# The memory's rows for its mean square: four pieces during RWKV instead of two loads during the memory's split

## The chip, the core and the metric

The kernel runs on one core of one Trainium2 chip. A core has five engines, each with its own instruction queue: TensorE (PE, matrix products; PEld is its weight load), VectorE (DVE), ScalarE (ACT), GpSimd (POOL) and SyncE (SP, which here issues most DMAs). They meet through semaphores. Sixteen DMA engines move data between the chip's memory (HBM) and the on-chip buffer (SBUF); products land in PSUM banks. The metric is the time of the device in microseconds (us), lower is better, as a median over runs.

## What is computed

Two transformer blocks over 256 tokens of width 2048. The first has four token mixers (gated DeltaNet, mLSTM, RG-LRU, RWKV-7) and a gated feed-forward; the second has three attention branches, one of which reads a memory `mem` of 256 rows. The part that the change touches is the norm of that memory, and what runs beside it:

```python
def rms_norm(x, w):                       # over the last axis, eps 1e-6
    return x * rsqrt(mean(x * x) + eps) * w

def second_block(x, mem, ...):
    mem_n = rms_norm(mem, norm_mem_g)     # (256, 2048)
    ...
    mkv = einsum('bmd,de->bme', mem_n, w_mem_kv)
    mk, mv = split(mkv, 2)

def mlstm(u, ...):
    qk, v, o_raw, i_raw, f_raw = split(u, ...)
    qk = silu(causal_conv(qk, conv_w))    # conv over time, width 4
    q, k = heads(qk)                      # 4 heads, k scaled by 128 ** -0.5
    ...                                   # gated attention in chunks, then a norm per head
```

RG-LRU needs `softplus(-lambda)`; RWKV-7 needs, for two halves of its heads, a unit triangular matrix inverted. The gate of RWKV is `sigmoid(g_lo) @ g2`, with `g2` of 128 by 512.

## The kernel before

**The projections set the order.** Nearly all of TensorE's work is weight blocks times activations in split precision: each weight is cut into a high part (`ringH`, made by ScalarE, L1362) and a low part (`ringL`, raw minus high, made by VectorE, L1983), and three products are added up (L682/L683, or L653 to L655). A weight unit of 1 MB comes by a DMA of SyncE (L3039) into one of 3 buffers `raw`; a half of 1024 columns goes into one of 4 slots of `ringH` and `ringL`. In this part a half lasts TensorE some 2.8 us. The blocks have names: `w0` to `w6` feed RWKV, `m0` to `m3` mLSTM, `g...` DeltaNet.

**The mixers are woven in.** Each engine runs a generator per stage (`norm`, `mem`, `rwkv`, `mlstm` and so on), and `course` advances them by so many projection steps for each `yield`. The leading engine records at which step each of its yields falls, and the other engines follow these records. So a stage with more yields moves all stages behind it in its lane to later projection steps, on every engine. During RWKV a second lane, `beside_rwkv`, runs at the same pace: `scan` with `mem` (the memory's split into `memSt`, stored to `mem_hold` in four DMAs of 1 MB by SyncE, L3090), then `fold`, `lambda`, `mlstm`.

**What the stages hold.** `fold` is the memory's mean square: GpSimd loads the memory's 256 rows (in `mem`, two DMAs of 1 MB, L2923) into `memk`, which lies in the buffer of RG-LRU's input `gU`; ScalarE squares each of the two 128 x 2048 tiles and adds them up (L1554); VectorE scales the sum (L2230), ScalarE takes the root (L1490), VectorE the reciprocal (L2233), TensorE spreads it over the partitions (L775), VectorE copies it out of PSUM (L2237). `lambda` is a chain of small VectorE operations (L2195 to L2218) on 128 x 4 values behind an absolute value and an exponential of ScalarE (L1562, L1564). `mlstm` is a convolution for Q and one for K (ScalarE taps L1679 and Silu L1684; VectorE three L2515 per head), then for each of four heads a broadcast (L1089) and a product K Q (L1098); ScalarE copies the first out (L1716), VectorE takes differences (L2543), ScalarE the exponential (L1719), VectorE masks it (L2546, L2547) and multiplies it by the product (L2550); then TensorE's L1107 and L1111, whose bank VectorE frees at L2566; in the end a norm (L885).

**RWKV** goes through two halves of its heads. In each: sigmoids (ScalarE L1618), decays (VectorE L2368 to L2386, ScalarE L1624 to L1627), a root (ScalarE L1588) and its reciprocal (VectorE L2333), a broadcast (TensorE L902), then products and five levels of the inversion (TensorE L841, then L849 and L854; VectorE L2296, L2304, L2309). The products of all these stages share a ring of four PSUM banks, `ps4` to `ps7`: whoever takes a bank waits until the product that was in it four takes earlier has been read. VectorE's first shift of RWKV (L2349) stands behind `e.wait_ge(s_mh[2], 16)` (L2344), the landing of the third store to `mem_hold`, since RWKV's scratch overwrites the `memSt` it is stored from. The drain of block `.m0` (ScalarE) and the two memsets of GpSimd (L2932, L2933) wait for both squares.

Of the kernel before, what the change touches and what calls it, by code (L numbers as in the profile page):

```python
# [254 lines left out]
def beside_rwkv(L):  # L255
    scan = L.stage("scan")
    next(scan)
    yield
    for _ in L.stage("mem"):
        next(scan, None)  # L260
        yield
    yield from scan
    yield from L.stage("fold")
    yield from L.stage("lambda")
    while not L.done("m0"):
        yield
    yield from L.stage("mlstm")
# [50 lines left out]
def program(nc, I, out):  # L318
    ctx = ExitStack()
    with ctx:  # L320
# [23 lines left out]
        def v2(o, n):  # L344
            return AR[:, o:o + n]
# [50 lines left out]
        s_c, s_an, s_i, s_p, s_h, s_w, s_w2, s_o = (sem(f"s_{n}") for n in ("c", "an", "i", "p", "h", "w", "w2", "o"))  # L396
        s_xr, s_m, s_w3 = ([sem(f"s_{n}{k}") for k in range(2)] for n in ("xr", "m", "w3"))
        s_mt = sem("s_mt")
        s_x = [sem(f"s_x{k}") for k in range(6)]
        s_first = [sem(f"s_first{k}") for k in range(3)]  # L400
# [44 lines left out]
        sqs = v3(GU, 16, T)  # L445
        memk = v3(GU, 2, D)
        wsm = v3(SC + 8192, 16, 16)
# [143 lines left out]
        def tensor(e, S, ring, lane):  # L591
# [176 lines left out]

            def fold(L):
                for _ in range(4):  # L770
                    yield
                e.wait_ge(*me_v.at("r"))
                b = take("me", "r")
                for tt in range(2):
                    t = m1(b[:, ts(tt)], rm[:, tt:tt + 1].broadcast_to([128, 128]), ident, tt == 0)  # L775
                t.then_inc(*me_p.tick("r"))
                for _ in range(2):
                    yield
# [544 lines left out]
            def attB(L):  # L1323
# [10 lines left out]
            course(lane(unit, {  # L1334
                "norm": norm, "gates": gates, "scan": scan, "fold": fold, "lambda": lam, "stat2": stat2, "mem": mem, "rwkv": rwkv, "mlstm": mlstm, "gdn": gdn,
                "rglru": rglru, **{f"mix{m}": split(4) for m in range(4)}, **{f"split1.{q}": split1(q) for q in range(4)},
# [3 lines left out]
        def scalar(e, S, ring, lane):  # L1340
# [23 lines left out]
            def drain(B):  # L1364
                tag, what, bk = B.tag, kind[B.tag], PS[2 * (B.n % 2):2 * (B.n % 2) + 2]
                e.wait_ge(*use.at(half_end[tag] - 1))
                if tag == ".m0":
                    e.wait_ge(*me_a.at("ss", 1))
                    for g in range(4):
                        e.wait_ge(s_mh[g], 16)  # L1370
# [179 lines left out]

            def fold(L):
                for tt in range(2):
                    e.wait_ge(s_m[tt], 16)
                    act(memk[:, tt, :], memk[:, tt, :], ACT.Square, accum_out=small[:, 116 + tt:117 + tt]).then_inc(  # L1554
                        *me_a.tick("ss", tt))
                    yield
                root(me_v, me_a, rm)
                yield
# [376 lines left out]
            def final(L):  # L1935
# [10 lines left out]
            course(lane(unit, {  # L1946
                "norm": norm, "scan": scan, "mem": mem, "fold": fold, "lambda": lam, "rwkv": rwkv, "mlstm": mlstm,
                "gdn": gdn, "rglru": rglru,
# [8 lines left out]
        def vector(e, S, ring, lane):  # L1957
# [267 lines left out]

            def fold(L):
                yield
                yield
                e.wait_ge(*me_a.at("ss", 1))
                tsc(rm, small[:, 116:118], 1.0 / D, 1e-6, MUL, ADD).then_inc(*me_v.tick("ms"))  # L2230
                yield
# [628 lines left out]
            def attB(L):  # L2860
# [6 lines left out]
            course(lane(unit, {  # L2867
                "norm": norm, "gates": gates, "scan": scan, "mem": mem, "fold": fold, "lambda": lam, "rwkv": rwkv, "mlstm": mlstm, "gdn": gdn, "rglru": rglru,
                **{f"mix{m}": split("mix", nS, lambda k: mix[:, k, :], range(4 * m, 4 * m + 4)) for m in range(4)}, "stat1": stat1,
# [6 lines left out]
        def gpsimd(e, S, ring, lane):  # L2876
            use, drain_a, drain_v, pool, nx_a, me_a = (S[n] for n in ("use", "drain_a", "drain_v", "pool", "nx_a", "me_a"))
            nx_p, me_v, nx_v, gd_p, gd_a, gd_v, rg_a, rg_v, ml_v, sp_v, at_v = (
                S[n] for n in ("nx_p", "me_v", "nx_v", "gd_p", "gd_a", "gd_v", "rg_a", "rg_v", "ml_v", "sp_v", "at_v"))
            tr_p, st_a, st_v = S["tr_p"], S["st_a"], S["st_v"]  # L2880
# [37 lines left out]

            def mem(L):
                yield  # L2920
                e.wait_ge(*nx_p.at("r"))
                for tt in range(2):
                    e.dma_start(memk[:, tt, :], I["mem_2"][0, ts(tt), :]).then_inc(s_m[tt], 16)  # L2923
                yield

            def fold(L):
                for _ in range(5):
                    yield
                e.wait_ge(*me_a.at("ss", 1))
                for g in range(4):  # L2930
                    e.wait_ge(s_mh[g], 16)
                e.memset(mU[:, :, 0:3], 0.0).then_inc(*pool.tick("mU"))  # L2932
                e.memset(gU[:, :, 0:3], 0.0).then_inc(*pool.tick("gU"))  # L2933
                yield

# [92 lines left out]

            course(lane(unit, {"begin": begin, "mem": mem, "fold": fold, "gdn": gdn, "rglru": rglru, "gains": gains, "xf": finals, **{f"split2.{q}": split2(q) for q in range(4)}, "mk": mk, "mv": mv, "xc": xc}))

# [182 lines left out]
```

## Time and profile before

| | us |
|---|---|
| median of 3 runs | 2418.83 |
| lowest and highest | 2418.06, 2420.80 |
| the profiled execution | 2422.39 |
| its span | 2420.60 |

| engine | busy us | share |
|---|---|---|
| TensorE | 2391.7 | 99% |
| VectorE | 1451.6 | 60% |
| ScalarE | 1131.5 | 47% |
| GpSimd | 104.1 | 4% |

The span goes from the first to the last instruction in the trace; the execution's own time is 1.8 us more. TensorE is busy nearly throughout, so what counts is the little time in which it waits, and what its matmuls cost while the chip grants it less than the full clock. In the profile's rows a wait is given with the instruction that ended it.

### The profile page before, as it was taken

Reading aid. Unit: us, or ns where it says so; the run is one execution under the profiler, and the core shown is the slowest. Engines: PE = TensorE matmul, PEld = TensorE weight load, DVE = VectorE, ACT = ScalarE, POOL = GpSimd, SP = SyncE. Lnnn points to the kernel's source line nnn. Section 1 sums busy time; section 2 is a strip of 40 time slices with the busy share of each in tenths; the row PEclk is TensorE's granted clock in tenths of the full one; section 3 lists DMA queues with packets and bytes.
Section 4 is the critical chain, followed back from the end, with each engine's and each line's share of the span. In section 5 each row is a group of like instructions: output and inputs, shape, how many; then the busy total and the mean of one; then the engine's idle time right before and its main releaser. Section 6 shows DMA issues by size and latency. Waiting matters only on the chain.

```text
span 2420.6 us, 32301 instructions
## 1 busy us (share of the span) xinstructions
PE 2391.7 (99%) x13432; PEld 1990.9 (82%) x13432; DVE 1451.6 (60%) x1860; ACT 1131.5 (47%) x1425; POOL 104.1 (4%) x81
## 2 busy tenths in 40 slices
PE   9999999999999999999999999999999999999998
PEld 7777888978888888888888888888888888888887
DVE  6777657678755555555555565555555655555555
ACT  6635435563554444434443464445444455444444
POOL 1000001320000000000000040000000000000000
PEclk9999999999999999999999999999999999999999
DMA  9633334645555555555555566555445544555564
GB/s 298 224 123 122 123 123 162 234 162 184 196 192 184 185 190 188 195 189 184 184 190 191 181 213 232 188 177 168 163 157 191 191 140 157 192 191 192 192 240 140
DMA packets 245329, 443.55 MB, mean 183 GB/s; under 512 B 7360, under 2 KB 72512, under 8 KB 242624
## 3 DMA queue, kind: packets, MB, share of 16 engines
q1 hardware_dynamic: 241984, 423.65, 53.2%
q0 software_dynamic: 2624, 17.30, 1.9%
q8 instruction: 107, 1.75, 0.3%
q10 hardware_dynamic: 576, 0.53, 0.1%
q14 instruction: 38, 0.31, 0.0%
HBM read 430.97 MB, written 10.49 MB: 182 GB/s over the span
## 4 chain that ended last, share of the span: by engine, by line
PE 95%; DVE 2%; ACT 1%; DMA 1%; issue 0%; SPq 0%; ACTq 0%; DVEq 0%
PE pp L653 25%; PE pp L655 24%; PE pp L654 24%; PE pp L682 8%; PE pp L683 4%; PE ps L612 2%; PE ps L1274 1%; PE ps L1288 1%; PE ps L801 1%; DVE ringL L1983 1%; DMA mem_hold<-memSt 1%; DMA raw<-in_w_in 0%; PE ps L854 0%; ACT ringH L1362 0%; PE pp L688 0%
## 5 line engine op out<-in xcount | busy, mean ns | idle before, releaser
L1983 DVE TENSOR_TENSOR ringL<-raw,ringH 128x1024 fp32r<-128x1024 f32 x779 | 963.3, 1243 | 687.8 <-ACT ringH L1362 686.3
L1362 ACT CAST ringH<-raw 128x1024 fp32r<-128x1024 f32 x779 | 814.6, 1050 | 994.9 <-PE pp L655 870.3
L653 PE MATMUL pp<-ringH,nS 128*128 128x512 f32 x1376 | 544.0, 395 | 1.1 <-DVE nS L2739 1.1
L655 PE MATMUL pp<-ringH,nS 128*128 128x512 f32 x1376 | 536.4, 390 | 0.0
L654 PE MATMUL pp<-ringL,nS 128*128 128x512 f32 x1376 | 535.9, 389 | 0.0
L682 PE MATMUL pp<-nS,ringH 128*128 128x512 f32 x992 | 367.9, 411 | 8.7 <-DVE ringL L1983 4.5
L655 PEld LDWEIGHTS pp<-ringH,nS 128*128 128x128 f32 x1376 | 258.3, 188 | 54.4
L653 PEld LDWEIGHTS pp<-ringH,nS 128*128 128x128 f32 x1376 | 258.5, 188 | 54.0 <-ACT AR L1423 1.2
L654 PEld LDWEIGHTS pp<-ringL,nS 128*128 128x128 f32 x1376 | 258.6, 188 | 51.3 <-issue 0.2
L683 PE MATMUL pp<-nS,ringL 128*128 128x256 f32 x992 | 281.4, 284 | 0.0
L653 PE MATMUL pp<-ringH,xS 128*128 128x512 f32 x704 | 277.2, 394 | 0.0
L654 PE MATMUL pp<-ringL,xS 128*128 128x512 f32 x704 | 275.2, 391 | 0.0
L655 PE MATMUL pp<-ringH,xS 128*128 128x512 f32 x704 | 274.8, 390 | 0.0
L682 PEld LDWEIGHTS pp<-nS,ringH 128*128 128x128 f32 x992 | 189.9, 191 | 58.9 <-DVE ringL L1983 7.0
L683 PEld LDWEIGHTS pp<-nS,ringL 128*128 128x128 f32 x992 | 190.8, 192 | 0.3 <-issue 0.2
L655 PEld LDWEIGHTS pp<-ringH,xS 128*128 128x128 f32 x704 | 132.1, 188 | 30.3
L653 PEld LDWEIGHTS pp<-ringH,xS 128*128 128x128 f32 x704 | 132.3, 188 | 28.3
L654 PEld LDWEIGHTS pp<-ringL,xS 128*128 128x128 f32 x704 | 132.3, 188 | 27.9
L653 PE MATMUL pp<-ringH,hS 128*128 128x512 f32 x352 | 139.9, 397 | 0.0
L654 PE MATMUL pp<-ringL,hS 128*128 128x512 f32 x352 | 138.9, 395 | 0.0
L655 PE MATMUL pp<-ringH,hS 128*128 128x512 f32 x352 | 138.9, 395 | 0.0
L2027 DVE TENSOR_TENSOR AR<-AR,pp 128x512 f32<-128x512 f32 x128 | 87.6, 687 | 37.5 <-PE pp L655 35.0
(406 smaller groups left out, 1951.5 us busy)
## 6 DMA issues: line engine op xcount, KB each, us to landing
raw<-in_w_in SPq DMA_DIRECT2D x189, 1024.0 KB, 5.1
raw<-in_ffn_w_gate SPq DMA_DIRECT2D x44, 1024.0 KB, 5.2
raw<-in_ffn_w_up SPq DMA_DIRECT2D x44, 1024.0 KB, 5.1
raw<-in_ffn_w_down SPq DMA_DIRECT2D x44, 1024.0 KB, 5.1
raw<-in_w_out SPq DMA_DIRECT2D x32, 1024.0 KB, 5.1
raw<-in_w_mem_kv SPq DMA_DIRECT2D x16, 1024.0 KB, 5.3
raw<-in_w_proj_a SPq DMA_DIRECT2D x8, 1024.0 KB, 5.0
raw<-in_w_proj_m SPq DMA_DIRECT2D x8, 1024.0 KB, 5.1
```

Source lines behind the costliest of these rows:

```text
L612: t = e.transpose(b[:, 128 * n:128 * n + 128], s, ident)
L653: mm(o, XH[:, ts(j)], WH, first, False)
L654: mm(o, XH[:, ts(j)], WL, False, False)
L655: t_of[0] = mm(o, XL[:, ts(j)], WH, False, last)
L682: mm(bk[j], WH[:, c], nS[:, k, :, :], first, False)
L683: t = mm(bk[j][:, T:2 * T], WL[:, c], XH, False, last)
L801: t = m1(o, lhs[c][:, n, :], rhs[c][:, n, :] if b is None else rhs[c][:, n, :, :], n == 0)
L1274: t = mm(b[:, ts(m - a)], qt, kt, m == a and r == 0, r == len(scores[m]) - 1)
L1288: t = mm(b[:, 0:values[m].shape[-1]], PT[:, ts(m)], values[m], m == 0, m == n - 1)
L1362: e.copy(ringH[:, h % NSPL, 0:nh * cols], raw[:, u % NRAW, h0 * cols:(h0 + nh) * cols]).then_inc(*hi.tick(h))
L1983: tt2(ringL[:, h % NSPL, o], raw[:, u % NRAW, h0 * cols:(h0 + nh) * cols], ringH[:, h % NSPL, o].bitcast(F32), SUB).then_inc(*lo.tick(h))
L2027: tt2(x, x, bk[b][:, :], ADD).then_inc(*drain_v.tick(*name))
```

## The change

The two loads of the memory's rows during `mem` go. A new stage `square` stands behind `lambda`, where `fold` stood ahead of it. In it GpSimd loads the rows in four pieces of 128 x 1024 (512 KB each), one after the other into the same place, the buffer that holds RWKV's gate weights `g2` and is free after their product. Each load waits for the square of the piece before. ScalarE squares four times 1024 columns in place of twice 2048. VectorE adds the two sums of each tile with one instruction more before it scales. GpSimd's memsets and the drain of `.m0` no longer wait for the squares. The stage has 20 yields on TensorE ahead of its broadcast, where `fold` had 4, so `mlstm` behind it starts later. SyncE's queue is the same in both kernels.

```diff
@@ def beside_rwkv(L):
     yield from scan
-    yield from L.stage("fold")
     yield from L.stage("lambda")
+    yield from L.stage("square")
     while not L.done("m0"):
         yield
     yield from L.stage("mlstm")
...
-        memk = v3(GU, 2, D)
+        memk = v2(SGo, 1024)
@@ TensorE
-            def fold(L):
-                for _ in range(4):
+            def square(L):
+                for _ in range(20):
                     yield
@@ ScalarE, drain of .m0
-                    e.wait_ge(*me_a.at("ss", 1))
+                    e.wait_ge(*nx_p.at("r"))
@@ ScalarE
-            def fold(L):
-                for tt in range(2):
-                    e.wait_ge(s_m[tt], 16)
-                    act(memk[:, tt, :], memk[:, tt, :], ACT.Square, accum_out=small[:, 116 + tt:117 + tt]).then_inc(
-                        *me_a.tick("ss", tt))
-                    yield
+            def squares_of_memory(L):
+                for n in range(4):
+                    for _ in range(4):
+                        yield
+                    e.wait_ge(s_m[n], 16)
+                    o = (116, 112)[n // 2] + n % 2
+                    act(memk, memk, ACT.Square, accum_out=small[:, o:o + 1]).then_inc(*me_a.tick("ss", n))
+                yield
+                yield
                 root(me_v, me_a, rm)
                 yield
@@ VectorE
-            def fold(L):
-                yield
-                yield
-                e.wait_ge(*me_a.at("ss", 1))
-                tsc(rm, small[:, 116:118], 1.0 / D, 1e-6, MUL, ADD).then_inc(*me_v.tick("ms"))
+            def square(L):
+                for _ in range(17):
+                    yield
+                e.wait_ge(*me_a.at("ss", 3))
+                tt2(rm, small[:, 116:118], small[:, 112:114], ADD).then_inc(*me_v.tick())
+                own(me_v)
+                tsc(rm, rm, 1.0 / D, 1e-6, MUL, ADD).then_inc(*me_v.tick("ms"))
+                yield
                 yield
@@ GpSimd
-            def mem(L):
-                yield
-                e.wait_ge(*nx_p.at("r"))
-                for tt in range(2):
-                    e.dma_start(memk[:, tt, :], I["mem_2"][0, ts(tt), :]).then_inc(s_m[tt], 16)
-                yield
-
-            def fold(L):
-                for _ in range(5):
-                    yield
-                e.wait_ge(*me_a.at("ss", 1))
+            def square(L):
+                e.wait_ge(*nx_p.at("r"))
                 for g in range(4):
                     e.wait_ge(s_mh[g], 16)
                 e.memset(mU[:, :, 0:3], 0.0).then_inc(*pool.tick("mU"))
                 e.memset(gU[:, :, 0:3], 0.0).then_inc(*pool.tick("gU"))
-                yield
+                for n in range(4):
+                    e.wait_ge(*(me_a.at("ss", n - 1) if n else rw_p.at("g2", 2)))
+                    c = slice(1024 * (n // 2), 1024 * (n // 2) + 1024)
+                    e.dma_start(memk, I["mem_2"][0, ts(n % 2), c]).then_inc(s_m[n], 16)
+                    for _ in range(4):
+                        yield
```

What this does to the order of the queues, at three places. Line numbers of the changed kernel are higher by 1 to 7 behind line 397, which is why one instruction bears two of them.

ScalarE's queue around the root (L1588, after L1592) of RWKV's first half; L1554 is the square, L1566 and L1568 belong to `lambda`. Before:

```order
78 L1554 ACTIVATE AR,small<-AR 128x2048
79 L1624 ACT_TABLE_LOAD
80 L1624 ACTIVATE AR<-AR 128x512
81 L1625 ACTIVATE AR<-AR 128x512
82 L1627 ACTIVATE AR<-AR 128x512
83 L1632 COPY AR<-ps5 128x512
84 L1588 ACT_TABLE_LOAD
85 L1588 ACTIVATE small<-small 128x8
86 L1362 CAST ringH<-raw 128x1024
87 L1554 ACTIVATE AR,small<-AR 128x2048
```

After:

```order
78 L1566 ACTIVATE small<-prm 128x4
79 L1568 ACT_TABLE_LOAD
80 L1568 ACTIVATE small<-small 128x4
81 L1628 ACTIVATE AR<-AR 128x512
82 L1629 ACTIVATE AR<-AR 128x512
83 L1631 ACTIVATE AR<-AR 128x512
84 L1636 COPY AR<-ps5 128x512
85 L1592 ACT_TABLE_LOAD
86 L1592 ACTIVATE small<-small 128x8
```

Both squares have left this place; the two small operations of `lambda` have moved up into it, and the decays use the table that these load.

ScalarE's queue from the sigmoids (L1618, after L1622) of RWKV's second half to its decays (L1624, after L1628); L1684, after L1688, is the Silu of mLSTM's Q convolution. Before:

```order
128 L1588 ACTIVATE small<-small 128x8
129 L1362 CAST ringH<-raw 128x1024 x4
130 L1613 ACTIVATE AR<-AR 128x512
131 L1618 ACT_TABLE_LOAD
132 L1618 ACTIVATE AR<-ps,prm 128x256 x4
133 L1423 ACTIVATE AR<-pp,small 128x512 x2
134 L1362 CAST ringH<-raw 128x1024 x2
135 L1624 ACT_TABLE_LOAD
136 L1624 ACTIVATE AR<-AR 128x512
```

After:

```order
123 L1688 ACT_TABLE_LOAD
124 L1688 ACTIVATE AR<-AR 128x256
125 L1363 CAST ringH<-raw 128x1024 x3
126 L1688 ACTIVATE AR<-AR 128x256
127 L1617 ACTIVATE AR<-AR 128x512
128 L1622 ACT_TABLE_LOAD
129 L1622 ACTIVATE AR<-ps,prm 128x256 x4
130 L1424 ACTIVATE AR<-pp,small 128x512 x2
131 L1363 CAST ringH<-raw 128x1024 x2
132 L1688 ACT_TABLE_LOAD
133 L1688 ACTIVATE AR<-AR 128x256
134 L1628 ACT_TABLE_LOAD
```

Two more table loads and three Silu passes of the Q convolution now stand here; before, this convolution lay ahead of all of it. Behind the last of these rows the root (L1588, after L1592) follows after four operations and a table load, as before.

TensorE's queue at an mLSTM head (L1089, L1098) in RWKV's second half, and the same of after (L1090, L1099); L841, L849 and L854 are L842, L850 and L855 of after. Before, from the head's first products to the next half of a projection:

```order
1160 L1089 MATMUL ps<-grow,cm 128x256
1161 L1098 MATMUL ps<-AR 128x256
1162 L1098 MATMUL ps<-AR 128x128
1163 L841 MATMUL ps<-AR 64x64 x16
1164 L682 MATMUL pp<-nS,ringH 128x512
```

Some steps later the head's last products (L1107, L1111) stand ahead of the pair that takes four banks:

```order
1184 L1107 MATMUL ps<-AR 128x256
1185 L1107 MATMUL ps<-AR 128x128
1186 L1111 MATMUL ps<-cm,AR 64x1 x6
1187 L849 MATMUL ps<-AR 64x32 x16
1188 L854 MATMUL ps<-AR 64x32 x16
```

After:

```order
1214 L1090 MATMUL ps<-grow,cm 128x256
1215 L1099 MATMUL ps<-AR 128x256
1216 L1099 MATMUL ps<-AR 128x128
1217 L850 MATMUL ps<-AR 64x32 x16
1218 L855 MATMUL ps<-AR 64x32 x16
```

The first two products of heads 2 and 3 stood ahead of L841, which takes two banks, and those of heads 0 and 1 outside the inversion; now those of all four heads stand ahead of L849 and L854, which take four. L1107 and L1111 have gone to the place ahead of L841.

## Rows read from the trace of the kernel before

A row of a timeline has the start, the duration, the engine, the line, the operation with out<-in and its shapes, and in brackets how long the engine was idle before it and what ended that. A row of waits has total us, times and the longest.

**Rows 1.** The page: the chain that ended last; the weight loads, median to landing.

```profile
PE 95%; DVE 2%; ACT 1%; DMA 1%; issue 0%; SPq 0%; ACTq 0%; DVEq 0%
...
raw<-in_w_in SPq DMA_DIRECT2D x189, 1024.0 KB, 5.1
```

**Rows 2.** The waits of TensorE, 60 to 90 us: total, times, longest.

```profile
PE pp L682 <- DVE ringL L1983: 4.1, 3, 2.7
```

**Rows 3.** VectorE in order of time: start, duration, instruction, idle before.

```profile
75.27 0.69 DVE L2349 TENSOR_TENSOR AR<-AR 128x512 f32<-128x512 f32 x1 [4.53 <-DMA mem_hold<-memSt]
```

**Rows 4.** The DMA issues of SyncE in order of time.

```profile
62.30 0.55 SPq L3090 DMA_DIRECT2D mem_hold<-memSt  x1
```

**Rows 5.** GpSimd in order of time, 44 to 150 us.

```profile
55.81 1.18 POOL L2923 DMA_DIRECT2D AR<-in_mem  x2
```

**Rows 6.** The DMA queues at 62 to 63 us; issues, median us to landing.

```profile
q0 software_dynamic: 22, 0.18, 44.0%
...
mem_hold<-memSt SPq DMA_DIRECT2D x1, 1024.0 KB, 12.9
```

**Rows 7.** Stretches: PE, PEld, DVE, ACT, POOL busy, clock, DMA, GB/s.

```profile
70.00:74.00 4.00, 4.00 (x22) 2.74 (x21) 0.74 (x4) 2.36 (x3) 1.77 (x1) 1.00 1.04 399
78.00:80.00 2.00, 1.93 (x7) 1.70 (x8) 1.96 (x5) 1.60 (x3) 0.00 (x0) 0.63 0.54 134
80.00:82.00 2.00, 2.00 (x8) 1.71 (x7) 1.96 (x5) 0.00 (x0) 0.00 (x0) 0.52 1.04 355
284.00:286.00 2.00, 2.00 (x8) 1.71 (x7) 1.19 (x1) 0.00 (x0) 0.00 (x0) 0.50 0.04 13
```

**Rows 8.** ScalarE in order of time, 96 to 128 us.

```profile
100.00 1.95 ACT L1554 ACTIVATE AR<-AR 128x2048 f32<-128x2048 f32 x1
...
105.51 1.28 ACT L1588 ACT_TABLE_LOAD   x1
106.81 0.21 ACT L1588 ACTIVATE small<-small 128x8 f32<-128x8 f32 x1
```

**Rows 9.** The waits of TensorE in later stretches of 30 us, and 270:315.

```profile
PE ps L902 <- DVE small L2333: 1.6, 1, 1.6
...
PE ps L964 <- DVE AR L2237: 1.3, 1, 1.3
...
PE ps L849 <- DVE AR L2296: 0.8, 1, 0.8
...
PE ps L902 <- DVE small L2333: 2.2, 1, 2.2
...
PE ps L854 <- DVE small L2566: 1.1, 2, 0.6
```

**Rows 10.** VectorE in order of time, 146 to 172 us.

```profile
157.81 1.53 DVE L2515 SCALAR_TENSOR_TENSOR AR<-AR,prm 128x256 f32<-128x256 f32 x3 [1.64 <-ACT AR L1679]
```

**Rows 11.** ScalarE, VectorE, TensorE in order of time, 156 to 232 us.

```profile
156.32 1.05 ACT L1362 CAST ringH<-raw 128x1024 fp32r<-128x1024 f32 x1 [4.80 <-PE pp L683]
...
160.29 0.42 ACT L1684 ACTIVATE AR<-AR 128x256 f32<-128x256 f32 x1
...
219.21 0.63 ACT L1613 ACTIVATE AR<-AR 128x512 f32<-128x512 f32 x1 [1.60 <-DVE AR L2368]
...
230.78 0.20 DVE L2333 RECIPROCAL small<-small 128x8 f32<-128x8 f32 x1 [2.23 <-ACT small L1588]
...
232.30 1.09 PE L902 MATMUL ps<-cm,small 128*64 128x128 f32 x16
```

**Rows 12.** TensorE and VectorE in order of time, around one mLSTM head.

```profile
274.09 0.59 PE L1089 MATMUL ps<-grow,cm 128*128 128x256 f32 x2
274.52 0.81 PE L1098 MATMUL ps<-AR 128*128 128x256 f32 x4
...
280.72 0.67 PE L849 MATMUL ps<-AR 64*64 64x32 f32 x32
...
276.80 0.56 DVE L2550 TENSOR_TENSOR AR<-AR,ps 128x384 f32<-128x384 f32 x1
```

More of the change, by code:

```diff
@@ L396, in program @@
         s_c, s_an, s_i, s_p, s_h, s_w, s_w2, s_o = (sem(f"s_{n}") for n in ("c", "an", "i", "p", "h", "w", "w2", "o"))
-        s_xr, s_m, s_w3 = ([sem(f"s_{n}{k}") for k in range(2)] for n in ("xr", "m", "w3"))
+        s_xr, s_w3 = ([sem(f"s_{n}{k}") for k in range(2)] for n in ("xr", "w3"))
         s_mt = sem("s_mt")
+        s_m = [sem(f"s_m{k}") for k in range(4)]
         s_x = [sem(f"s_x{k}") for k in range(6)]
@@ L1334, in tensor @@
             course(lane(unit, {
-                "norm": norm, "gates": gates, "scan": scan, "fold": fold, "lambda": lam, "stat2": stat2, "mem": mem, "rwkv": rwkv, "mlstm": mlstm, "gdn": gdn,
+                "norm": norm, "gates": gates, "scan": scan, "lambda": lam, "square": square, "stat2": stat2, "mem": mem, "rwkv": rwkv, "mlstm": mlstm, "gdn": gdn,
                 "rglru": rglru, **{f"mix{m}": split(4) for m in range(4)}, **{f"split1.{q}": split1(q) for q in range(4)},
@@ L1946, in scalar @@
             course(lane(unit, {
-                "norm": norm, "scan": scan, "mem": mem, "fold": fold, "lambda": lam, "rwkv": rwkv, "mlstm": mlstm,
+                "norm": norm, "scan": scan, "mem": mem, "lambda": lam, "square": squares_of_memory, "rwkv": rwkv, "mlstm": mlstm,
                 "gdn": gdn, "rglru": rglru,
@@ L2867, in vector @@
             course(lane(unit, {
-                "norm": norm, "gates": gates, "scan": scan, "mem": mem, "fold": fold, "lambda": lam, "rwkv": rwkv, "mlstm": mlstm, "gdn": gdn, "rglru": rglru,
+                "norm": norm, "gates": gates, "scan": scan, "mem": mem, "lambda": lam, "square": square, "rwkv": rwkv, "mlstm": mlstm, "gdn": gdn, "rglru": rglru,
                 **{f"mix{m}": split("mix", nS, lambda k: mix[:, k, :], range(4 * m, 4 * m + 4)) for m in range(4)}, "stat1": stat1,
@@ L2877, in gpsimd @@
             use, drain_a, drain_v, pool, nx_a, me_a = (S[n] for n in ("use", "drain_a", "drain_v", "pool", "nx_a", "me_a"))
-            nx_p, me_v, nx_v, gd_p, gd_a, gd_v, rg_a, rg_v, ml_v, sp_v, at_v = (
-                S[n] for n in ("nx_p", "me_v", "nx_v", "gd_p", "gd_a", "gd_v", "rg_a", "rg_v", "ml_v", "sp_v", "at_v"))
+            nx_p, rw_p, me_v, nx_v, gd_p, gd_a, gd_v, rg_a, rg_v, ml_v, sp_v, at_v = (
+                S[n] for n in ("nx_p", "rw_p", "me_v", "nx_v", "gd_p", "gd_a", "gd_v", "rg_a", "rg_v", "ml_v", "sp_v", "at_v"))
             tr_p, st_a, st_v = S["tr_p"], S["st_a"], S["st_v"]
@@ L3027, in xc @@
                 yield
-            course(lane(unit, {"begin": begin, "mem": mem, "fold": fold, "gdn": gdn, "rglru": rglru, "gains": gains, "xf": finals, **{f"split2.{q}": split2(q) for q in range(4)}, "mk": mk, "mv": mv, "xc": xc}))
+            course(lane(unit, {"begin": begin, "square": square, "gdn": gdn, "rglru": rglru, "gains": gains, "xf": finals, **{f"split2.{q}": split2(q) for q in range(4)}, "mk": mk, "mv": mv, "xc": xc}))
         def sync(e, S, ring, lane):
```

## The prediction, made before the changed kernel ran

> **What bounds the kernel now.** The page first: TensorE is busy in 2391.7 us of a span of 2420.6, as the table above says, and has 95% of the chain that ended last [rows 1]. So an edit on another engine counts only where TensorE waits for that engine, or where the chip grants TensorE less than its full clock. The second view is therefore TensorE's waits, stretch by stretch through the part that the change touches, up to 315 us. The reader is to see that they are few and short: 4.1 us before 90 us, and behind that single ones of 0.8 to 2.2 us [rows 2, 9]. The third view is the granted clock of stretches [rows 7]: at 78 to 82 us it is 0.63 and 0.52 of full, right behind TensorE's longest wait, and 0.50 at 284 to 286 us, one of three such spells between 283 and 307 us. The last view is the order of the queues, since the change moves far more than it adds.
>
> **The stall at 78 us.** The longest of TensorE's waits, 2.7 us, is for `ringL` of L1983 [rows 2]. What held VectorE is one row: L2349 began at 75.27 us after 4.53 us of idling for a store to `mem_hold` [rows 3], and both splits stand behind it in VectorE's queue. The store is the third; SyncE issued it at 62.30 us [rows 4] and it took 12.9 us to land, while the software queue, which holds nothing but the memory's two loads (issued from 55.81 us on [rows 5]), had 44% of the DMA engines' time beside it [rows 6]. The engines were full (share 1.04 at 399 GB/s in 70 to 74 us [rows 7]), so 2 MB less in front are 2.1 / 0.399 = 5.3 us. The third store then lands near 70, when VectorE gets there (75.27 - 4.53 = 70.74 us), and its wait goes. TensorE gets back 2.7 us. Next late is nothing that I see: the raw halves wait in the same full queue and come earlier too. Of the other 1.4 us of [rows 2] I take nothing: they are backlog of ScalarE and VectorE. The slow spell behind it costs (1 - 0.63) x 2 + (1 - 0.52) x 2 = 1.7 us [rows 7]. I take it as caused by the wait and count it: **-4.4 us**, bounds -2.7 (the spell stays) and -4.4.
>
> The Trainium skill ("DMA: Bandwidth & Descriptors", section "SWDGE vs HWDGE vs iDMA") says that software and hardware queues feed different queues inside each DMA engine, which takes them in turn. The 44% of [rows 6] agrees. By that rule the loads delay the store as by the row's estimate, so it leaves the sum as it is.
>
> **The first root.** L902 waits 1.6 us for VectorE's reciprocal [rows 9], which waits for ScalarE's root at 106.81 us [rows 8]. Ahead of it ScalarE has the first square of 1.95 us. It goes; `lambda`'s two operations come, of about 0.2 us each like the small root [rows 8], and their table serves the decays, so no load is added: -1.95 + 0.4 = **-1.5 us** (bounds -1.6, the whole wait, and 0). The second square stands behind the root and holds nobody.
>
> **The broadcast.** L964 waits 1.3 us for VectorE's copy L2237, which frees the bank of the memory's broadcast [rows 9]. It moves to near 192 us: **-1.3 us** (0 if it finds a new neighbour at once, since L775's bank must be freed there too).
>
> **Squares and pieces at their new place.** ScalarE's work is 4 x about 1.0 us, half of 1.95. It falls between 146 and 186 us, where ScalarE idles for TensorE between casts, 4.80 us in one place [rows 11]. Each piece of 512 KB is issued behind one square and needed some 10 us later at the next, four yields on; SyncE's weight loads of twice the size land in a median of 5.1 us [rows 1]. Cost 0; without that cover a late piece would hold the casts behind it, and at most 4 x 1.0 = 4 us would reach TensorE. GpSimd's queue has the waits for the squares in front of its products for RWKV and mLSTM; it is busy 4% of the span. VectorE's one instruction more costs 0.2 us, hidden.
>
> **VectorE in 150 to 210 us.** `lambda` and the Q convolution leave. The convolution is three L2515 of together 1.53 us per head [rows 10]; they and `lambda` stand in front of L2296, for which L849 waits 0.8 us: **-0.8**. The wait of 2.2 us near 209 us (the fourth row of [rows 9]), for the norm of RWKV's first half, has K's convolution in front. It shrinks, but its own chain of sums, root and reciprocal stays: I take **-0.9**, bounds -2.2 and 0. Gains together: 4.4 + 1.5 + 1.3 + 0.8 + 0.9 = **-8.9 us**.
>
> **The second root, the first loss.** The Q convolution now meets RWKV's second half. In front of the root ScalarE gets two more table loads, each with a Silu: 2 x (1.28 + 0.42) = 3.4 us [rows 8, 11]. Its Silu waits for VectorE's three L2515, two groups of which fall here: 2 x 1.53 = 3.1. Sum 6.5. ScalarE idles 1.60 us in front of L1613 [rows 11], of which I take 1.0 as usable: the chain comes 5.5 us later. L2333 ended at 230.98, L902 began at 232.30 without a wait: slack 1.3. **+4.2 us**, bounds 3.4 - 1.6 - 1.3 = 0.5 and 6.5 - 1.3 = 5.2.
>
> The Trainium skill ("ScalarE: Activation LUTs", "What ACT_TABLE_LOAD costs") adds a drain of about 1.38 us to each switch. The row speaks against it: the load of 105.51 us is 1.28 and the next activation starts at 106.81 [rows 8]. With that rule the loss would be an estimated 2 x 1.38 = 2.8 us more.
>
> **Behind it.** K's convolution, three L2515 before each Silu, stands near 254 to 268 us beside casts. I take 1.0 us for one split L1983 that has to stand behind a group of 1.53 with little slack. L841 needs ScalarE's copy L1579, now queued behind a Silu that waits for such a group and behind its 0.42 us: 1.7 us. **+2.7**, bounds 0 and 2.7.
>
> **The heads.** Where L1089 and L1098 stand ahead of L849 and L854, L854 takes the banks of the head's two products (six takes on a ring of four). The later is free when L2550 ends, 276.80 + 0.56 - 274.09 = 3.27 us after L1089 began [rows 12]. TensorE fills of this up to the end of L1098 274.52 + 0.81 - 274.09 = 1.24, and L849's 0.67: it waits 1.36 us. Four heads: 5.4. Gone is what before had at this place, L854 for L2566, 1.1 us [rows 9]. **+4.3 us**, bounds 2.6 (the chain as short as its instructions' sum, 2.9 us) and 5.4.
>
> **Sum.** -8.9 + 4.2 + 2.7 + 4.3 = +2.3 us on 2422.39. That execution lies 3.56 us above the median of 2418.83, so 2418.83 + 2.3 = **2421.1 us**. The clock of the later part I leave as it is, three slow spells before and three after. This is the loosest term: each costs 1.7 us, and they stand near TensorE's waits, which move.
>
> **Rivals.** *Covered* (faster): the convolution finds ScalarE and VectorE idle, so that the second root costs 0.5, the 2.7 are nothing and the heads cost 2.6. Two of the three slow spells go, since the waits that they follow are gone: -8.9 + 0.5 + 2.6 - 3.4 = -9.2, **2409.6 us**; with the spells kept 2413. For it: VectorE is busy only 60%. Against: in both chains each engine waits for the other, and idle shares don't help there. *Spells* (slower): the four waits of 1.36 us in the heads, each beside small products, each bring a slow spell; from two more on, with the second root at 5.2, this decides: 2.3 + 3.4 + 1.0 = +6.7, **2425.5 us**. For it: the two spells that I could set beside a wait follow it at once [rows 2, 7, 9]. *The store is not what is late*: with it earlier, VectorE waits as long for ScalarE's casts, and TensorE still stalls at 78 us: +4.4, **2425.5 us**. Against: VectorE's wait names the DMA, 4.53 us [rows 3]. *The drain* of the page above: **2423.9 us**.
>
> **Chances.** Forecast 0.44, covered 0.27, spells 0.22, store 0.05, drain 0.02. What can be told from no change is 0.2%, 4.8 us: below 2414.0 is faster, above 2423.7 slower. The forecast's own range is 2417 to 2425 and puts 0.07 of its 0.44 above. Covered gives 0.26 of faster, the forecast 0.01; spells 0.20, store 0.05, drain 0.01 and the 0.07 make slower 0.33; same has the other 0.40. The range 2411 to 2428 takes in all but about half of the covered case and a rest of spells.
>
> **What would show it.** Right: L2349 without its wait for `mem_hold` and a clock of 1.00 at 74 to 80 us; L902 near 100 us and L964 without waits; L902 near 225 us with 3 to 5 us of wait; L855 waiting four times for L2550's line. Wrong: a second L902 with under 1 us, casts that wait for a square or a piece, or a number of slow spells other than three behind 230 us.

## The result, and the profile after

| | before | changed |
|---|---|---|
| median | 2418.96 us (13 runs) | 2424.76 us (13 runs) |
| lowest to highest | 2417.04 to 2420.80 | 2422.08 to 2430.00 |
| profiled execution | 2422.39 | 2422.93 |
| TensorE's waits, 30 to 350 us | 13.2 us | 16.1 us |

The ratio is 1.0024, 95% interval 1.0016 to 1.0031; a second set of runs gave 1.0028 (1.0018 to 1.0038). So the kernel became slower by 5.8 us, just over what can be told from no change. The two profiled executions differ by only 0.5 us. That of before (2422.39 us) is slower than its kind, that of the changed kernel (2422.93 us) faster than its own. The mean granted clock of an execution says why: 0.996 and 0.997 in these two, but 0.9967 in the mean of 68 runs of the kernel before and 0.9955 in that of the 13 runs of the changed one. Such a mean is the better measure of the clock than one profile, since each profile catches other slow spells (stretches in which the granted clock is half). In the table, the sum of waits is that of all rows of TensorE's waits from 30 to 350 us; behind 350 us TensorE waits 2.8 us in the one kernel and 2.9 in the other.

TensorE's waits of the changed kernel, in order of the stretches 60:90, 90:120, 180:210, 210:240, 240:270, 270:300 and 300:330, answer to [rows 2] and [rows 9] (line, what it waited for, total, times, longest). 120 to 180 us, where before waited 2.3 us, has none:

```profile
PE pp L683 <- DVE ringL L1987: 1.4, 2, 1.0
...
PE ps L943 <- DVE small L2337: 0.7, 1, 0.7
...
PE ps L903 <- DVE small L2340: 1.4, 1, 1.4
...
PE ps L903 <- DVE small L2340: 2.3, 1, 2.3
PE pp L683 <- DVE ringL L1987: 1.2, 2, 0.8
PE ps L943 <- DVE small L2337: 0.4, 1, 0.4
...
PE ps L842 <- ACT AR L1583: 0.4, 1, 0.4
...
PE ps L855 <- DVE AR L2557: 3.9, 2, 2.2
...
PE ps L855 <- DVE AR L2557: 3.1, 2, 1.6
PE ps L886 <- ACT AR L1694: 1.3, 1, 1.3
```

The third and the fourth row are two different waits here, at 201.6 and 228.2 us.

**The stall at 78 us.** VectorE's L2356 (L2349 of before) began at 72.09 us after 1.14 us of idling for a product of GpSimd, not at 75.27 after 4.53 us for the store [rows 3]:

```profile
72.09 0.69 DVE L2356 TENSOR_TENSOR AR<-AR 128x512 f32<-128x512 f32 x1 [1.14 <-POOL AR L2903]
```

The third store landed in 8.9 us, not 12.9 [rows 6]:

```profile
mem_hold<-memSt SPq DMA_DIRECT2D x1, 1024.0 KB, 8.9
```

It was issued at 62.50 us, so it came at 71.4. GpSimd's product (from 70.22 us on, 1.77 us long) ended at 71.99, later than the store.

And the granted clock at 78 to 82 us is full, where it was 0.63 and 0.52 [rows 7]; there is a slow spell instead at 275 us, right behind the first long wait of the heads:

```profile
78.00:80.00 2.00, 2.00 (x17) 1.86 (x16) 2.00 (x4) 1.86 (x3) 0.00 (x0) 1.00 0.73 252
80.00:82.00 2.00, 2.00 (x14) 1.78 (x14) 1.96 (x4) 0.01 (x1) 0.00 (x0) 1.00 0.58 143
274.00:280.00 6.00, 5.57 (x49) 4.98 (x50) 2.74 (x6) 0.10 (x1) 0.00 (x0) 0.72 0.29 102
```

**The first root.** ScalarE's root (L1592) starts at 101.64 us, with `lambda`'s table load and exponential (L1568) where the square was [rows 8]:

```profile
96.79 1.28 ACT L1568 ACT_TABLE_LOAD   x1
98.09 0.20 ACT L1568 ACTIVATE small<-small 128x4 f32<-128x4 f32 x1
...
100.35 1.28 ACT L1592 ACT_TABLE_LOAD   x1
101.64 0.21 ACT L1592 ACTIVATE small<-small 128x8 f32<-128x8 f32 x1
```

L903 (L902 of before) doesn't wait here any more; L943 ahead of it waits 0.70 us for L2337, with which VectorE reads the sums of squares out of their PSUM bank.

**The pieces.** GpSimd issued them at 129.01, 141.22, 154.76 and 166.57 us, and ScalarE squared them (1.05 us each, and 0.19 to read the sum) at 139.77, 153.32, 165.13 and 176.07, without waiting for one. GpSimd's product at 144.70 waited for VectorE, not for a square:

```profile
129.01 0.58 POOL L2935 DMA_DIRECT2D AR<-in_mem  x1
141.22 0.54 POOL L2935 DMA_DIRECT2D AR<-in_mem  x1 [11.63 <-ACT AR L1558]
144.70 1.30 POOL L2908 TENSOR_TENSOR AR<-AR 128x512 f32<-128x512 f32 x1 [2.94 <-DVE AR L1995]
```

**The second root.** ScalarE in 213 to 228 us, to be read against [rows 11]. The Silu at 213.37 waited 3.87 us for L2522 (the convolution, L2515 of before), the one at 222.52 0.71 us, with a table load ahead and another behind; the root came at 227.70 us:

```profile
213.37 0.42 ACT L1688 ACTIVATE AR<-AR 128x256 f32<-128x256 f32 x1 [3.87 <-DVE AR L2522]
...
220.53 1.28 ACT L1688 ACT_TABLE_LOAD   x1
222.52 0.42 ACT L1688 ACTIVATE AR<-AR 128x256 f32<-128x256 f32 x1 [0.71 <-DVE AR L2522]
...
227.70 0.21 ACT L1592 ACTIVATE small<-small 128x8 f32<-128x8 f32 x1
```

**The heads.** L855 waited four times for L2557 (L2550 of before), the first time 2.21 us, which answers to [rows 12]:

```profile
274.43 1.46 PE L855 MATMUL ps<-AR 64*64 64x32 f32 x32 [2.21 <-DVE AR L2557]
```

In this first head ScalarE's exponential (L1723, L1719 of before) has a table load in front:

```profile
271.35 1.28 ACT L1723 ACT_TABLE_LOAD   x1
272.65 0.52 ACT L1723 ACTIVATE AR<-AR 128x384 f32<-128x384 f32 x1
```

### The profile page after: what moved, and what is told of

It reads as the page before. It is cut to its first block, busy times and chain, and to the rows that moved or that the text cites. A ratio compares the mean times of both kernels' runs of the same rounds, so it can differ in the third digit from the quotient of the medians.

```text
span 2421.1 us, 32310 instructions
## 1 busy us (share of the span) xinstructions
PE 2389.2 (99%) x13432; PEld 1988.6 (82%) x13432; DVE 1451.8 (60%) x1861; ACT 1134.3 (47%) x1431; POOL 107.5 (4%) x83
## 4 chain that ended last, share of the span: by engine, by line
PE 92%; DVE 4%; ACT 2%; issue 1%; DMA 0%; POOL 0%; SPq 0%; ACTq 0%; POOLq 0%; DVEq 0%
PE pp L654 25%; PE pp L656 24%; PE pp L655 24%; PE pp L683 7%; PE pp L684 3%; PE ps L613 2%; DVE ringL L1987 1%; PE ps L1275 1%; PE ps L1289 1%; PE ps L802 1%; DVE AR L2522 1%; DMA raw<-in_w_in 0%; PE ps L855 0%; PE pp L689 0%; PE pp L690 0%
```

## The experiments

Each line of the table is a kernel that was run; the texts on record stand below it. "Waits" are TensorE's from 30 to 350 us in the profiled execution, less those of before (13.2). Ratios are to the kernel before on the same chip. "Clock" is the mean granted clock of all runs of that kernel; beside the 0.9967 of the kernel before (68 runs), a difference of 0.0010 is 0.0010 x 2419 = 2.4 us.

| kernel | waits, us | clock (runs) | ratio (95% interval) | times 2419 us |
|---|---|---|---|---|
| changed | +2.9 | 0.9955 (13) | 1.0024 (1.0016, 1.0031) | +5.8 |
| mlstm_later | +7.7 | 0.9938 (5) | 1.0060 (1.0047, 1.0074) | +14.5 |
| heads_late_five | +5.0 | 0.9940 (5) | 1.0044 (1.0032, 1.0057) | +10.6 |
| heads_late_six | -0.5 | 0.9965 (11) | 0.9997 (0.9988, 1.0006) | -0.7 |
| heads_shifted | -3.2 | 0.9973 (11) | 0.9983 (0.9974, 0.9992) | -4.1 |
| loads_later | -0.4 | 0.9969 (11) | 0.9996 (0.9987, 1.0005) | -1.0 |
| loads_after_stores | -2.1 | 0.9971 (11) | 0.9985 (0.9976, 0.9994) | -3.6 |
| square_last | -5.6 | 0.9971 (11) | 0.9981 (0.9973, 0.9990) | -4.6 |
| square_beside | -5.2 | 0.9965 (6) | 0.9970 (0.9959, 0.9981) | -7.3 |

Waits and clock together give the times of the first seven within 1 us: the changed kernel's +5.8 is 2.9 of waits and (0.9967 - 0.9955) x 2419 = 2.9 of clock. The last two are off by 2.0 and 2.5 us. In square_last the squares fall behind 350 us, where TensorE waits 6.3 us in place of 2.9; for square_beside the rest stays open.

### mLSTM moved, and nothing else

```diff
@@ before: def beside_rwkv(L)
     yield from L.stage("lambda")
+    yield from L.stage("pause")      # 16 empty yields on TensorE
     while not L.done("m0"):
         yield
```

> The kernel before, with 16 empty yields between lambda and mlstm and nothing else changed: the loads, the squares and lambda stay where they were, mLSTM's convolutions and heads go where the change puts them. Theory (the place of mLSTM is what costs): the stall at 78 us, the wait of L902 near 107 us and of L964 near 127 us stay; the waits in 150 to 210 us shrink by 1.7 us; then the second root (+4.2), the convolution of K (+2.7) and the heads (+4.3, TensorE waiting four times for L2550) come, so +8 to +10 us on the kernel before, 2427 to 2429 us. Rival (the squares and pieces at their new place are what costs): no change, 2417 to 2421 us.

Measured: 2433.87 us, +14.5. Its main waits:

```profile
PE ps L859 <- DVE AR L2555: 6.9, 4, 2.2
PE ps L907 <- DVE small L2338: 5.2, 3, 2.3
PE pp L683 <- DVE ringL L1988: 4.7, 4, 2.4
```

L859 and L907 are L854 and L902 of before. The stall and the first root's wait have stayed as before, the waits of the heads and of the second root have come. So the place of mLSTM costs, alone, more than the whole change; the theory holds and its size was too small. Of the 14.5 us only 7.7 are waits; the clock of its five runs, 0.9938 against 0.9967, makes up the other 7.0.

The waits in 150 to 210 us shrank by 0.95 us, not by 1.7 as expected. L907's went from 2.15 to 1.37 us, so K's convolution was in front of it. The one of 0.8 us (L849 of before, L854 here) stayed, though the Q convolution had left. In front of L2296, for which it waits, stand five small instructions of `lambda`, the first at 151.21 us, one of them 1.20 us long. In square_beside, further down, a group of the Q convolution stands in that place and nothing waits. VectorE of before:

```profile
151.48 1.20 DVE L2215 TENSOR_TENSOR small<-small 128x4 f32<-128x4 f32 x1
...
152.86 0.75 DVE L2296 TENSOR_TENSOR AR<-ps,AR 128x256 f32<-128x256 f32 x2
```

And of square_beside:

```profile
149.47 1.53 DVE L2526 SCALAR_TENSOR_TENSOR AR<-AR,prm 128x256 f32<-128x256 f32 x3
151.03 0.76 DVE L2307 TENSOR_TENSOR AR<-ps,AR 128x256 f32<-128x256 f32 x2
```

### The heads alone, at two places half a level apart

```diff
@@ before: mlstm, on TensorE, ScalarE and VectorE, ahead of the loop over the heads
+                for _ in range(5):      # 6 in heads_late_six
+                    yield
                 for h in range(4):
```

> The kernel before with 5 empty yields ahead of mLSTM's heads alone; loads, squares, lambda and both convolutions stay. The heads stand as in the changed kernel, L1089 and L1098 ahead of L849 and L854 of four levels of the inversion. Theory (banks): TensorE waits 6 to 7 us for L2550 where it waited 1.1 for L2566 and 0.3 at L1107, so +5.2 us without the clock, and if slow spells follow such waits, one to two more of 1.7 us in the mean: 2424 to 2428 us. Rival (the second root and the convolutions are the whole loss, the heads' waits only take the place of others): 2419 to 2421 us.

> The same with 6 yields in place of 5: all four heads stand one half of a level later, L1089 and L1098 ahead of L841, L1107 and L1111 ahead of L849 and L854. Theory (banks, not lateness): three or four waits of 0.55 us for L2566 and no long one, 2419 to 2421 us, within 1 us of the kernel before and 5 us or more below the kernel with 5 yields. Rival (heads that come late cost, wherever they stand): 2424 us or more, as with 5 yields.

Measured: 2431.60 us, above the 2424 to 2428 expected, against 2419.73 us. The two differ in one yield. With five, the waits and the stretch 250:350 (busy times, then the granted clock, the DMA share and GB/s):

```profile
PE ps L854 <- DVE AR L2556: 6.9, 4, 2.2
...
250.00:350.00 100.00, 91.82 (x1102) 78.55 (x1101) 58.57 (x113) 34.38 (x46) 6.03 (x5) 0.95 0.33 103
```

With six:

```profile
PE ps L854 <- DVE small L2572: 1.6, 3, 0.5
...
250.00:350.00 100.00, 97.25 (x1196) 82.60 (x1195) 64.34 (x123) 37.49 (x50) 6.99 (x6) 1.00 0.38 120
```

The waits answer as expected: 6.9 us for L2556 (L2550 of before) against 1.6 for L2572 (L2566). The heads that stand later, but on the right side, cost nothing. The times differ by 11.9 us, though, and the waits by 5.5. In the profiled executions the granted clock of 250 to 350 us is 0.95 against 1.00, which is (1 - 0.95) x 100 = 5 us, and the mean clock of all runs, 0.9940 against 0.9965, gives 6 us. So the long waits of the heads and the norm behind them cost, taken together, about as much again by the clock.

### The changed kernel with its heads half a level later

```diff
@@ changed: mlstm, on TensorE, ScalarE and VectorE, ahead of the loop over the heads
+                yield
                 for h in range(4):
```

> The changed kernel with one yield more ahead of mLSTM's heads on TensorE, ScalarE and VectorE: a head's first products (L1089, L1098) stand ahead of L841 again, its last ones (L1107, L1111) ahead of L849 and L854. Theory (in the changed kernel L854 waits for the banks of both products, 7.0 us in the four heads by its trace): these waits go, three of about 0.55 us for L2566 come as before the change: -5.3 us on the changed kernel, 2419 to 2420 us. If slow spells of the clock follow those waits, their number falls too and the runs spread less than 2422 to 2430 us, and the gain is up to 7 us. Rival (the wait only moves to the next product that needs a bank or to the norm behind the heads): 2423 to 2426 us.

Measured: 2415.74 us, 0.17% under the kernel before, and spread over 4.1 us, not 7.9. The waits of the heads:

```profile
PE ps L855 <- DVE small L2576: 1.6, 3, 0.5
```

One yield turns the change from +5.8 to -4.1 us. The waits are 6.1 us less, and the mean clock rises from 0.9955 to 0.9973, which is 4.4 us. The first theory's bound of 7 us was too small, the rival falls. Because two sets of runs are compared here, both kernels were run once more side by side:

> The changed kernel as it is, on the same chip as the next two, for its clock in a second profiled execution. Its waits are the same as in the first (16.1 us between 30 and 350 us); the theory that long waits in the heads bring slow spells expects 3 or more of them behind 200 us and a median 5 to 6 us over the kernel before. If the first set of runs was only unlucky with the clock: 2 to 3 us over it.

> The changed kernel with one yield more ahead of the heads, a second time, beside the changed one. Waits 6.1 us less; the theory expects 8 to 10 us less in the median, the surplus by the clock; if the clock has nothing to do with the waits, 6 us less.

Measured: 2425.72 and 2416.19 us, 9.5 us apart. The clock of the changed kernel in its second profiled execution:

```profile
250.00:350.00 100.00, 91.23 (x1074) 77.71 (x1073) 62.63 (x128) 37.45 (x54) 6.00 (x5) 0.95 0.32 101
```

It is 0.95 again as in the first (0.97 and 0.98 in the two of the shifted one). Its slow stretches began at 274.3, 301.6 and 328.9 us, in the first execution at 275.0, 302.3 and 329.6. In the first, waits for L2557 and L1694 end at 274.4, 301.7 and 326.9 us. So three slow spells fall behind the same three waits in both, and the waits of 288.9 and 316.0 us had none in either.

That stretch alone favours the theory, though. From 200 to 250 us the changed kernel has a clock of 1.00 in both profiled executions, the shifted one 0.97 and 0.93: its L903 waits the same 2.3 us for the second root, and there a slow spell stands beside the wait (228.8 and 227.2 us), where the changed kernel has none. From 30 to 350 us all four executions lose the same to the clock, 5.1 us. What shows a surplus over the waits is the whole set of runs: 9.5 us in the medians for 6 us of waits, and mean clocks of 0.9955 and 0.9949 against 0.9973 and 0.9965. Which spells of the unprofiled runs make it up isn't shown.

### The stall at 78 us alone

```diff
@@ before: GpSimd, mem
-                yield
+                for _ in range(7):
+                    yield
                 e.wait_ge(*nx_p.at("r"))
+                e.wait_ge(s_mh[2], 16)
```

> The kernel before, with the memory's two loads of 1 MB issued only when the third store to mem_hold has landed (near 70 us), all else as before. Theory (the loads beside the stores make the stall): VectorE's wait for mem_hold falls from 4.5 us to under 1, TensorE's wait at 78 us goes, and so does the spell at half clock behind it: -2.7 to -4.4 us, 2414 to 2416 us; the squares at 100 us still find their data. Rival (the third store is late for another reason, or VectorE would wait for ScalarE instead): the wait at 78 us stays at over 2 us and the time at 2417 to 2421 us.

Measured: 2418.80 us, no change that can be told. VectorE's wait for the store is gone and another is in its place:

```profile
DVE AR L2349 <- POOL AR L2896: 2.9, 1, 2.9
```

GpSimd's product for RWKV (L2896) stood behind the load's wait for the store, in the same queue. TensorE's wait at 78 us still fell from 2.7 to 1.0 us and the clock of 70 to 90 us is 1.00, but 1.2 us of new waits came elsewhere, 1.0 of them at the first root. Waits (-0.4) and that spell (-1.7) would make -2.1 us; measured is -1.0, within -3.1 and +1.2. So this edit was no clean test; the next one moves the loads behind GpSimd's fourth product, with no wait:

```diff
@@ before: GpSimd
-            def mem(L):
-                yield
+            def scan(L):
+                for _ in range(10):
+                    yield
                 e.wait_ge(*nx_p.at("r"))
```

> The kernel before with the two loads issued near 78 us, behind GpSimd's fourth product for RWKV and with no wait for a store in GpSimd's queue. In the run that held them for the third store, VectorE's L2349 waited 2.9 us for GpSimd's product, which stood behind that wait, in place of 4.5 for the store, and TensorE's waits fell by only 0.4 us in all. Theory (the gain was hidden by that): TensorE's longest wait at 78 us falls under 0.5 us, the wait of L902 near 105 us grows by up to 1 us since ScalarE's square sets it; waits in all 1 to 2.5 us less, 2417 to 2418.5 us. Rival (the stall is worth its 2.7 us and a slow spell in full): 2415 us. Rival (it is worth nothing alone): 2419 to 2420 us.

Measured: 2416.47 us, ratio 0.9985 (0.9976 to 0.9994). Its waits for the root and the ring:

```profile
PE ps L902 <- DVE small L2333: 4.3, 2, 2.1
PE pp L682 <- DVE ringL L1983: 1.4, 2, 1.1
```

The wait at 78 us is gone (1.4 us are left, as in the changed kernel), and L902 waits 4.3 us in its two places where it waited 3.7. The clock of 70 to 90 us is 1.00 in all kernels without the stall, and 0.91 in all four that have it. So 2.7 us of waits went with the stall, and 0.6 came back at the first root. The waits fell by 2.1 us, as the theory had it; the time, at 2416.47 us, is a little under its range of 2417 and lies between it and the rival's 2415. The interval (-5.8 to -1.5 us) holds both, so the spell's 1.7 us are seen in the clock of the stretch but not told apart in the time.

### The squares and pieces at another place

```diff
@@ changed: def beside_rwkv(L), square_last; GpSimd's two memsets in a stage of their own, clear
     yield from L.stage("lambda")
-    yield from L.stage("square")
+    yield from L.stage("clear")
     while not L.done("m0"):
         yield
     yield from L.stage("mlstm")
+    yield from L.stage("square")
```

```diff
@@ square_last: the last two stages, square_beside
-    yield from L.stage("mlstm")
-    yield from L.stage("square")
+    squares = L.stage("square")
+    for _ in L.stage("mlstm"):
+        next(squares, None)
+        yield
+    yield from squares
```

> The changed kernel with the stage of the squares behind mlstm in place of ahead of it (GpSimd's memsets stay ahead of mlstm): pieces and squares at 300 us and later, mLSTM where it was before the change. Theory: the gains up to 200 us stay (8.1 us by the trace, less up to 1.7 us, since the convolutions stand in 150 to 210 us again), the losses behind 210 us go: 2411 to 2413 us. Rival (the losses belong to the pieces and squares, or to lambda's earlier place): 2418 us or more.

> The changed kernel with the squares' stage drawn in the same yields as mlstm in place of ahead of it: pieces and squares stand at 150 to 200 us as in the changed kernel, mLSTM where it stood before. Theory (pieces and squares at that place are free, only mLSTM's move costs): as with the squares at the end, 2413 to 2416 us. Rival (they hold ScalarE's casts and Silus beside the convolutions, or GpSimd's products for mLSTM wait behind the squares): 2418 us or more, with waits of TensorE for ringL or for L2515's followers between 150 and 210 us.

Measured: 2414.43 us, above the 2411 to 2413 expected, and 2412.74 us. The first has new waits behind 350 us, as said under the table. The second keeps the squares at 158.6 to 189.5 us, among mLSTM's convolutions; the intervals of the two ratios overlap. Its main waits:

```profile
PE ps L907 <- DVE small L2344: 2.2, 1, 2.2
PE pp L687 <- DVE ringL L1991: 1.4, 2, 1.0
PE ps L890 <- ACT AR L1698: 1.1, 1, 1.1
PE ps L859 <- DVE small L2577: 1.1, 2, 0.5
```

L907, L890 and L859 are L902, L885 and L854 of before. These four were there before the change; new are 0.7 us at L943 and 0.4 at L885. So no wait is left that a square or a piece brings at that place, and the loss is mLSTM's move. A second set beside the changed kernel:

> The changed kernel with the squares beside mlstm, a second time. If its first result (ratio 0.997, six runs) holds: 0.996 to 0.998 of the kernel before, 11 to 13 us under the changed one, of which 8.1 us are waits (16.1 against 8.0).

Measured: 2412.56 us, ratio 0.9969 (0.9956 to 0.9981), 13.2 us under the changed kernel (2425.72) on the same chip. Its waits are 9.4 us, not the 8.0 of the first profile: at 218.9 us TensorE waits for VectorE's copy of the memory's broadcast (L2248, L2237 of before). So the broadcast can still cost at its new place, in one of the two executions. This wait, and the clock of 250 to 350 us:

```profile
PE ps L890 <- DVE AR L2248: 1.2, 1, 1.2
...
250.00:350.00 100.00, 96.67 (x1181) 81.58 (x1181) 60.29 (x119) 34.90 (x48) 5.90 (x5) 1.00 0.37 117
```

This kernel beats both the one before and the changed one: it has the change's gains, and mLSTM where it was.

## Why the prediction came out as it did

The time was forecast at 2421.1 us, within 2411 to 2428, and measured at 2424.8. The direction was right, the size was not: +2.3 forecast, +5.8 measured. By its steps, in us:

| step | forecast | waits measured |
|---|---|---|
| stall at 78 us | -2.7 | -2.7 |
| first root | -1.5 | -1.55 + 0.70 at L943 = -0.85 |
| broadcast, L964 | -1.3 | -1.3 |
| L849, L854 | -0.8 | -1.0 |
| L902 near 209 us | -0.9 | 1.36 - 2.15 = -0.8 |
| second root | +4.2 | 0.80 + 0.40 + 2.30 = +3.5 |
| behind it | +2.7 | 0.39 + 0.44 = +0.8 |
| heads | +4.3 | 7.0 - 1.1 = +5.9 |
| other waits near the heads (L1107, L854 for L2587, the norm) | 0 | -0.33 - 0.81 + 0.39 = -0.75 |
| all waits | +4.0 | +2.9 |
| clock | -1.7 (the spell at 78 us) | +2.9 in the mean of the runs |

**Right, with its mechanism.** The stall went because two loads less stood beside the store, and loads_after_stores shows it alone. The store came 4.0 us sooner, not 5.3, and something was next late, GpSimd's product, but not late enough to bring TensorE's wait back. The broadcast came as read from one row. K's convolution was in front of the wait near 209 us, as mlstm_later shows. The second root came later behind two table loads and the convolution's groups, as its rows show; it cost 3.5 us, of which 2.3 are at L903 itself, where 3 to 5 had been named as the sign. The pieces and squares were hidden, as the run with them beside the convolutions shows. The table load of 100.35 us is followed by the activation at 101.64, so no drain is to be seen; the Trainium skill ("ScalarE: Activation LUTs", "What ACT_TABLE_LOAD costs") adds one of about 1.38 us, and the trace of neither kernel bears it out here.

**Right number, wrong reason.** L849's 0.8 us were put down to `lambda` and the Q convolution together. It was `lambda` alone, as mlstm_later and square_beside show.

**Wrong in size.** The first root's gain was half given back, because the sums of L943 became what is late (that L902 would be free was right). "Behind it" was sized at 2.7 and was 0.8: I had placed a whole group of L2515 in front of a split and of L1579, and most of it fell into idle time. The heads' waits were sized at 1.36 us each and were 2.21, 1.71, 1.56 and 1.56. The chain from L1089 to the end of L2550, taken at 3.27 us, held in heads 1 to 3 (3.25 to 3.40 us). L855 starts 0.15 us behind its end, and TensorE's own work under it is 1.84 us and not 1.91: that makes 1.56. In head 0 a table load of 1.28 us lies in the chain, which the rows of a later head could not show. The lower bound of this term doesn't come out of the chain of 2.9 us that it names: 4 x (2.9 - 1.24 - 0.67) - 1.1 = 2.9, not 2.6. It would put the covered case 0.3 us higher.

**Luck.** The sum of waits came near by errors that cancel: the heads 1.6 us too low, the first root 0.65 too high in gain, "behind it" 1.9 and the second root 0.7 too high, and three small waits near the heads (-0.75 in all) not taken at all.

**The step that failed**, though the time fell in the stated range, is "The clock of the later part I leave as it is, three slow spells before and three after". The waits add up to +2.9 us, where the forecast had +4.0, and +2.3 with its clock term. The clock was taken to give 1.7 us back and took 2.9 (0.9955 against 0.9967 in the mean of the runs), so the clock term missed by 4.6 us; the waits, 1.1 us under their forecast, hid some of that, and 3.5 us of miss are left. As a count the step held in the profiles: three spells behind 230 us in both executions of the changed kernel. What was wrong is the number that they were set against. The sum starts from the median, 2418.83 us, but the three spells of before stand in the profiled execution of 2422.39 us, 3.56 us above it, which is what two spells of 1.7 us cost. Eight other profiled executions, of kernels with no long wait in the heads, have no spell in 250 to 350 us (two), one (five) or two (one). So a median run of before has probably fewer than three there. That is inferred, since only one execution of before was profiled.

What was written of the rival "Spells" gave 2425.5 us, within 1 us of the measurement, and had a chance of 0.22. Its direction is what happened, and the clock of the heads is shown by the pair with five and six yields: 5.5 us of waits, 11.9 us of time. That its number fits is luck in part: it took the second root at 5.2 us, which was 3.5, and a spell for each of the four waits, where two of them had none in either profile.

**What was not settled.** Slow spells are not the same in each execution: square_beside had one in 250 to 350 us in its first profile and none in its second. Why one wait brings a spell and an equal one does not is open. The mean clock of the runs says how much was lost, but not behind which waits.

## What to carry to other kernels

A stage that is put into a lane moves everything behind it: here the moved loads gained what was read from them, and the yields around them lost more, most of it by setting mLSTM's heads against the wrong half of an inversion level. Count the banks of a shared ring at each place where two stages meet, since one yield earlier or later was worth 9 to 12 us. And where TensorE is 99% busy, price a group of waits, in the mean over runs, at 1.6 to 2.2 times their length: 11.9 us for 5.5 of waits (five and six yields), 9.5 for 6.1 (one yield in the changed kernel), 14.5 for 7.7 (mLSTM moved). For a single wait this says nothing, since equal waits came with and without a spell. And take the clock of the kernel before from many runs, not from the one that was profiled.

## What the runs showed of the chip

- The granted clock fell to half beside single waits of 0.55 to 2.7 us, though TensorE is busy 99% of the span. In the thirteen profiled executions all 34 spells between 30 and 350 us begin during such a wait or at most 2.9 us behind its end; a spell cost 1.7 us, two of them twice that. Kernels with the four long waits had 0.95, 0.95, 0.95 and 0.91 in 250 to 350 us; those without had 0.97 to 1.00, but the kernel before, with waits of 0.55 and 0.91 us, had 0.95 in its one profiled execution.
- The length of a wait doesn't decide it. The wait of 2.30 us for the second root brought a spell in heads_shifted (twice) and mlstm_later and none in the changed kernel (twice); that of some 2.2 us near 205 us brought one in four executions of eight.
- Whether such a spell comes varies between executions, and so does the time: the changed kernel's 13 runs spread over 7.9 us, with a mean granted clock of 0.996 to 0.997 in the four fastest and 0.992 and 0.994 in the two slowest. In the mean of all runs the four sets with the long waits had 0.9938 to 0.9955, all others 0.9965 to 0.9973.
- A store of 1 MB beside two loads from another queue took 12.9 us, without them 8.9.
